# Block 0 of the input projection: raw x tiles transposed as they land, its tokens' norm factors applied behind PSUM, w_in rows loaded by halves

## What is computed

```python
def rmsnorm(x, g):
    r = lax.rsqrt(jnp.mean(xf * xf, axis=-1, keepdims=True) + EPS)
    return (xf * r * g).astype(x.dtype)

h = rmsnorm(x, norm1_g)
z = h @ w_in
za = z[..., :A_WIDTH]      # four Fourier heads
zb = z[..., A_WIDTH:]      # four pooling groups, windows 2, 4, 8, 16
```

## Time and profile before

| | us |
|---|---|
| median of 3 runs | 2491.86 (2491.79 to 2493.97) |
| profiled execution, device time | 2491.23 |
| its span in the trace | 2489.4 |
| PE busy | 2474.7 (99%) |
| DVE busy | 1676.6 (67%) |
| ACT busy | 965.2 (39%) |
| POOL busy | 166.9 (7%) |

### The profile page before, as it was taken

The page is one execution under the profiler, slowest core; times in us unless marked ns, Lnnn a source line. Parts: engine busy times, 40 slices in busy tenths (PEclk is TensorE's granted clock), DMA queues, the critical chain, the costliest instruction groups (busy, mean ns, idle before and its releaser), DMA issues.

```text
span 2489.4 us, 32156 instructions
## 1 busy us (share of the span) xinstructions
PE 2474.7 (99%) x11141; PEld 2049.1 (82%) x11141; DVE 1676.6 (67%) x2600; ACT 965.2 (39%) x1830; POOL 166.9 (7%) x222
## 2 busy tenths in 40 slices
PE   9999999999999999999999999999999999999998
PEld 7888878887888888888888888888888888888887
DVE  5555788779767767877677687666774564455565
ACT  5534566667333333433333343333332232233333
POOL 2555400000000000000000000000000000000000
PEclk9999999999999999999999999999999999999999
DMA  6433767666423222532232432232346654354554
GB/s 184 115 85 99 223 221 254 238 238 260 157 80 116 97 103 110 195 113 110 80 126 101 155 146 96 110 110 89 118 186 217 242 200 168 119 196 149 195 189 148
DMA packets 154373, 381.99 MB, mean 153 GB/s; under 512 B 11992, under 2 KB 48184, under 8 KB 145076
## 3 DMA queue, kind: packets, MB, share of 16 engines
q1 hardware_dynamic: 145616, 350.81, 40.8%
q0 software_dynamic: 8240, 29.94, 3.2%
q10 hardware_dynamic: 432, 0.14, 0.0%
HBM read 254.22 MB, written 126.62 MB: 153 GB/s over the span
## 4 chain that ended last, share of the span: by engine, by line
PE 85%; DVE 2%; ACT 1%; issue 0%; DMA 0%; DVEq 0%
PE bank L351 28%; PE bank L353 28%; PE bank L352 28%; PE bank L2020 1%; ACT a_hi L2401 0%; DVE a_lo L2592 0%; DMA a_raw<-ha_scr 0%; PE bank L1373 0%; PE bank L1059 0%; DVE x L1818 0%; ACT h_out L1637 0%; DVE scratch L1033 0%; DVE zy_late L1044 0%; DVE uv_lo L1071 0%; ACT xn L1627 0%
## 5 line engine op out<-in xcount | busy, mean ns | idle before, releaser
L351 PE MATMUL bank<-a_hi,w_hi 128*128 128x512 f32 x1848 | 719.4, 389 | 2.0 <-DVE w_lo L2603 1.6
L352 PE MATMUL bank<-a_lo,w_hi 128*128 128x512 f32 x1848 | 718.9, 389 | 0.0
L353 PE MATMUL bank<-a_hi,w_lo 128*128 128x512 f32 x1848 | 718.9, 389 | 0.0
L351 PEld LDWEIGHTS bank<-a_hi,w_hi 128*128 128x128 f32 x1848 | 346.9, 188 | 75.6 <-DVE w_lo L2603 2.8
L353 PEld LDWEIGHTS bank<-a_hi,w_lo 128*128 128x128 f32 x1848 | 347.0, 188 | 72.0
L352 PEld LDWEIGHTS bank<-a_lo,w_hi 128*128 128x128 f32 x1848 | 347.0, 188 | 71.7
L351 PE MATMUL bank<-t_hi,s_hi 128*128 128x512 f32 x924 | 359.4, 389 | 0.0
L352 PE MATMUL bank<-t_lo,s_hi 128*128 128x512 f32 x924 | 359.4, 389 | 0.0
L353 PE MATMUL bank<-t_hi,s_lo 128*128 128x512 f32 x924 | 359.4, 389 | 0.0
L2414 ACT ACTIVATE w_hi<-t_raw 128x512 fp32r<-128x512 f32 x256 | 162.3, 634 | 462.4 <-PE bank L353 378.8
L2753 DVE TENSOR_TENSOR s_lo<-s_raw,s_hi 128x512 fp32r<-128x512 f32 x231 | 156.2, 687 | 230.7 <-ACT s_hi L2489 230.7
(11 more groups left out here) (277 smaller groups left out, 3163.1 us busy)
## 6 DMA issues: line engine op xcount, KB each, us to landing
s_scr<-sums_out SPq DMA_DIRECT2D x33, 1792.0 KB, 5.9
s_raw<-s_scr SPq DMA_DIRECT2D x42, 1024.0 KB, 5.0
w_raw<-in_w_gate SPq DMA_DIRECT2D x64, 512.0 KB, 3.5
w_raw<-in_w_up SPq DMA_DIRECT2D x64, 512.0 KB, 4.3
wd_staged<-in_w_down SPq DMA_DIRECT2D x121, 256.0 KB
a_raw<-ha_scr SPq DMA_DIRECT2D x21, 1024.0 KB, 5.0
s_raw<-s_scr SPq DMA_DIRECT2D x21, 768.0 KB, 4.4
x<-in_x SPq DMA_DIRECT2D x24, 512.0 KB, 4.9
```

Source lines behind the costliest of these rows:

```text
L351: pe.matmul(out, w_hi, m_hi, start=first, stop=False, **checks)
L352: pe.matmul(out, w_hi, m_lo, start=False, stop=False, **checks)
L353: return pe.matmul(out, w_lo, m_hi, start=False, stop=last, **checks)
```

## The change

The tiles of block 0 are transposed as they land, without a factor. Each token's factor is applied to z when it leaves PSUM: DVE does this in `first_staged`, in place of ACT's `stage_z(0, c)`. Since a token is a column there, the 512 factors must lie along the free dimension on all partitions: POOL stores `rstd` to a scratch in DRAM and loads it back to all partitions as `rstd_row`. The rows of w_in are loaded by halves, all the pooling halves first, then all the Fourier halves, then x block 1. DVE rounds the first pooling row in ACT's place. Of block 1, ACT scales two quarters in place of one. The squares of tile 3 move behind step d = 1 and the chain of `rstd` behind d = 4.

```diff
         for d in range(KT):
-            sp.dma_start(w_raw[:, d, :], w_rows[d // ROWS, d % ROWS]).then_inc(ahead.row_loaded[d], DMA)
-            if d == 5:
-                load_x(1, 1)
+            sp.dma_start(w_raw[:, d, HALF:], w_rows[d // ROWS, d % ROWS, :, HALF:]).then_inc(ahead.row_loaded[d], DMA)
+        for d in range(KT):
+            sp.dma_start(w_raw[:, d, 0:HALF], w_rows[d // ROWS, d % ROWS, :, 0:HALF]).then_inc(mixed_loaded, DMA)
+        load_x(1, 1)
         sp.dma_start(edges[:, :], edge).then_inc(edge_loaded, DMA)
+        sp.wait_ge(squares_done, 4)
         sp.wait_ge(transposed, KT)
...
+        pool.wait_ge(rstd_chain, 4)
+        pool.dma_start(rstd_scr.rearrange("(p t) -> p t", p=P), rstd[:, 0, :]).then_inc(rstd_moved, DMA)
+        pool.wait_ge(rstd_moved, DMA)
+        pool.dma_start(rstd_row[:, :], rstd_scr.partition_broadcast(P)).then_inc(rstd_moved, DMA)
         pool.wait_ge(edge_loaded, DMA)
...
-        first_squares()
+        for t in range(3):
+            first_squares(t)
+        act.wait_ge(constants_made, GAIN_MADE)
         for d in range(KT):
-            act.wait_ge(ahead.row_loaded[d], DMA)
-            act.activation(w_hi[:, POOLED, d, :], w_raw[:, d, HALF:].rearrange("p (g e) -> p g e", g=4),
-                           ACT.Copy).then_inc(w_hi_done, 1)
...
+            if d:
+                act.wait_ge(ahead.row_loaded[d], DMA)
+                if d == 1:
+                    act.wait_ge(w_hi_done, 1)
+                act.activation(w_hi[:, POOLED, d, :], w_raw[:, d, HALF:].rearrange("p (g e) -> p g e", g=4),
+                               ACT.Copy).then_inc(w_hi_done, 1)
             round_h(0, 0, d, first=True)
+            if d == 1:
+                first_squares(3)
+            if d == 3:
+                act.wait_ge(var_ready, 1)
+                act.activation(std[:, 0, :], var[:, 0, :], ACT.Sqrt).then_inc(std_ready, 1)
-        stage_z(0, 0, first=True)
         for k in range(KT):
             round_folded(k)
             if k < 6:
-                squares(1, 2 * ROWS * DMA, 1, range(4 + 2 * k, 6 + 2 * k))
-            else:
-                stage_z(0, k - 5, first=True)
-        stage_z(0, 3, first=True)
+                squares(1, 2 * ROWS * DMA, 1, range((0, 3, 6, 9, 12, 14)[k], (3, 6, 9, 12, 14, 16)[k]))
...
+        def first_staged(c):
+
+            dve.wait_ge(z_ready, c + 1)
+            if c == 0:
+                dve.wait_ge(rstd_moved, 2 * DMA)
...
+            ps, row = by_tile(z_ps[c % 4][:, :]), rstd_row[:, :].rearrange("q (p t) -> q t p", t=4)
+            if c >= HEADS:
+                h = c - HEADS
+                if h >= 2:
+                    dve.wait_ge(z_stored[h - 2], DMA)
+                dve.tensor_tensor(by_tile(z_out[:, h % 2, :]), ps, row, ALU.mult).then_inc(z_staged, 1)
+                return
+            staged = dve.tensor_tensor(by_tile(zb[:, c, 2 * PAD:2 * PAD + HALF]), ps, row, ALU.mult)
+            if c:
+                staged = dve.scalar_tensor_tensor(out=by_tile(zk[:, c - 1, PAD:WIDE]), in0=ps, scalar=float(WINDOWS[c]),
+                                                  in1=row, op0=ALU.mult, op1=ALU.mult)
+            staged.then_inc(z_staged, 1)
...
         copy_turned(0)
+        first_staged(0)
         for k in range(KT):
             if k + 1 < KT:
                 copy_turned(k + 1)
             rest_of_folded(k)
-        step(0, 0, quarters=3)
+            if k + 1 < HEADS:
+                first_staged(k + 1)
+        first_step()
...
         pe.wait_ge(warm_ready, 2)
-        pe.wait_ge(x_first[0], DMA)
-        warm_up(4)
+        warm_up(7)
         pe.wait_ge(const_loaded, DMA)
...
+        for t in range(4):
+            pe.wait_ge(x_first[t], DMA)
             for d in range(4):
...
                 mm = pe.transpose(t_ps[d][:, t * P:(t + 1) * P], every_fourth(xin[0][:, t, :], d), eye[:, :])
+                if t == 3:
+                    mm.then_inc(transposed, 1)
+            if t == 1:
+                pe.wait_ge(constants_made, DMA)
+                for r in range(ROWS):
...
+            if t:
+                warm_up(1)
```

More of the change, by code:

```diff
@@ L371, in every_fourth, with project_in @@
     return ap.rearrange("p (s j r) -> p s r j", s=2, r=ROWS)[:, d // ROWS, d % ROWS]
-def project_in(nc, ctx, ahead, mixer, pooled, x, w_in, g1, ident, z_scr, table, channel, edge):
+def project_in(nc, ctx, ahead, mixer, pooled, x, w_in, g1, ident, z_scr, rstd_scr, table, channel, edge):
     NJ = TOKENS // HALF
@@ L493, in scalar, with first_squares @@
     def scalar(act):
[L494 to L504, removed]
+        def first_squares(t):
+            act.wait_ge(x_first[t], DMA)
+            if t:
+                act.wait_ge(squares_done, t)
+            act.activation(junk[:, :], xin[0][:, t, :], ACT.Square,
+                           accum_out=sumsq[:, 0, t:t + 1]).then_inc(squares_done, 1)
         def squares(j, loads, slot, blocks=range(NBLK)):
@@ L530, in stage_z @@
                     act.wait_ge(z_stored[h - 2], (j + 1) * DMA)
-                elif not first:
+                else:
                     act.wait_ge(z_stored[h + 2], j * DMA)
@@ L535, in stage_z @@
             g = c
-            if not first:
-                act.wait_ge(ahead.group_done, j * 4 + (g - 3))
+            act.wait_ge(ahead.group_done, j * 4 + (g - 3))
             staged = act.activation(zb[:, g, 2 * PAD:2 * PAD + HALF], z_ps[c % 4][:, :], ACT.Copy)
@@ L657, in rest_of_folded, with step @@
                               w_hi[:, MIXED, k, :].bitcast(F32), ALU.subtract).then_inc(w_ready, 1)
-        def step(j, slot, quarters=4):
-            norm(j + 1, 1 - slot, quarters)
+        def step(j, slot):
+            blocks_variance(j + 1)
+            blocks_scale(j + 1, 1 - slot, 4)
             for d in range(3):
@@ L666, in step, with first_step @@
                     turn(j + 1, 1 - slot, d + 3)
+        def first_step():
+            blocks_variance(1)
+            first_staged(HEADS)
+            blocks_scale(1, 1, 2)
+            for d in range(3):
+                turn(1, 1, d)
+                if d == 1:
+                    first_staged(HEADS + 1)
+            for d in range(KT):
+                rest_of_h(1, 1, d)
+                if d + 3 < KT:
+                    turn(1, 1, d + 3)
+                if d == 3:
+                    first_staged(HEADS + 2)
+            first_staged(HEADS + 3)
         dve.memset(warm[:, 0:1], 1.0).then_inc(warm_ready, 1)
         dve.memset(ahead.still[:, :].bitcast(F32), 0.0).then_inc(warm_ready, 1)
[L670 to L675 removed]
         dve.wait_ge(constants_made, GAIN_TURNED)
@@ L680, in vector @@
                             ).then_inc(constants_made, 1)
+        dve.wait_ge(ahead.row_loaded[0], DMA)
+        dve.tensor_copy(w_hi[:, POOLED, 0, :], w_raw[:, 0, HALF:].rearrange("p (g e) -> p g e", g=4)).then_inc(w_hi_done, 1)
         dve.wait_ge(constants_made, GAIN_MADE)
@@ L747, in turn_w @@
         def turn_w(k):
+            if k == 0:
+                pe.wait_ge(mixed_loaded, (KT + 1) * DMA)
             if k < 2:
@@ L3023, in encoder @@
         pooled = Pooled(ahead, y_scr)
-        front = project_in(nc, ctx, ahead, mixer, pooled, x, w_in, g1, ident, z_scr, table, channel, edge)
+        front = project_in(nc, ctx, ahead, mixer, pooled, x, w_in, g1, ident, z_scr, rstd_scr, table, channel, edge)
         mixing = mix(nc, ctx, ahead, mixer, z_scr, y_scr, w_pool)
```

91 lines of the change are left out of this document (36 added, 55 removed).

## The result

The changed kernel takes 2495.44 us (median of 22 runs, 2492.83 to 2498.81) against 2492.39 us for the kernel before (22 runs, 2490.98 to 2494.83): ratio 1.0013, 95% interval 1.0007 to 1.0019. It is 3.05 us slower, where the forecast stood at -0.15 against a baseline of 2491.86; the measured time lies 0.4 us above the range given. The difference is under the 0.2% that was named as the bound of "same", yet its interval excludes zero.

A forecast was written before the change was run, and what follows sets the result against it. PE's unbroken matmul stream was taken as the bound. Terms -2.45 + 2.3 + 0 + 0 = -0.15 against the profiled 2491.23 gave 2491.1, or 2491.7 in the median's terms; range 2489.2 to 2495.0 us.

The forecast's parts named there:

- What bounds the kernel: Whole span: one unbroken PE matmul stream, busy 99%, so only the first product's start and later holes decide.
- Part 1: Start: transposes without the norm bring the first product from 13.56 to 10.8; -2.45 us, from -3.65 to -0.35.
- floor of 9.9: Start: earliest first product, set by tile 3 alone and row 0's copy; 9.9, or -3.65.
- rival (c): Start: PE is slow at its first products; -0.35 + 2.3, 2493.8 us; chance 0.13.
- Part 2: Folds: DVE staging pair at 1.28 us delays fold 2 by 1.28, then two slips of 0.5; +2.3 us.
- break-even of 1.34 a pair: Folds: staging pair price above which the sum of fold slips and the start's -2.45 exceeds zero.
- Part 3: Factors' way through DRAM: two POOL DMAs at 3.0 us each land by 25.7, 8 us of cover; cost 0.
- Part 4: first_step of block 1: chain grows by 1.45 us, some 1.7 returns from POOL's earlier groups; 0, or +1.2 without return.
- The rule on GpSimd: Staged operations, bank and row, are free of POOL's contention; if false, 0.4 each, up to 2 us more.
- (b): Folds: staged pair costs more than it looks, counted three times; +3.65, 2495.5 us at doubled price; chance 0.12.
- signs of being wrong: Folds show no hole, the pair costs above 2 us, or the first product stays behind 12.
- the floor of part 1: Start: part 1's best case, -3.65 us, said to be left out of the range.

The follow-up runs named there:

- warm10: Changed kernel with ten dummy matmuls in place of seven ahead of the transposes; 2494.39 us, ratio 1.0007 to the kernel before.
- x_behind_warm: x_behind_store with ten dummy matmuls in place of seven; 2489.45 us, ratio 0.9989 to the kernel before.
- start_alone: Changed kernel with ACT copying z out of PSUM as before, block 0's factors and their DMAs left out; 2489.19 us, ratio 0.9990 to the kernel before.
- hole_filled: Changed kernel with dummy matmuls (7, 4 and 4) ahead of folds 2, 3 and 4; 2496.79 us, ratio 1.0013 to the kernel before.
- row_flat: Changed kernel reading the factors from adjacent words instead of every fourth, so they go to wrong tokens; 2492.38 us, ratio 1.0001 to the kernel before.
- x_behind_store: both_mended with x block 1 loaded only once the factors' store has landed; 2491.07 us, ratio 0.9993 to the kernel before.
- factors_first: both_mended with x block 1's load issued only when both factor DMAs have landed; 2492.34 us, ratio 0.9995 to the kernel before.
- both_mended: folds_mended with block 1's scaling put before the fifth group's staging in first_step; 2491.51 us, ratio 0.9992 to the kernel before.
- changed_again: Changed kernel unaltered, run again for a second profile; 2496.06 us, ratio 1.0011 to the kernel before.
- staging_alone: Kernel before with only DVE's staging by first_staged, using a row of ones; 2497.89 us, ratio 1.0024 to the kernel before.
- folds_mended: Changed kernel with one DVE staging operation per group, ACT making zk, three of four staged before the folds; 2492.18 us, ratio 1.0000 to the kernel before.

## Why the forecast was wrong

**What bounds the kernel** held. PE is busy 99% of the span, and up to the last `row_sums` the difference of every version is found in its start and its holes. Behind that mark all programs are the same, and the profiles need 2270.7 to 2272.6 us there (2274.3 in the first of the changed kernel). With such a scatter in single executions the medians follow the marks only to 1 or 2 us.

**Part 1** was right in mechanism, too large in this kernel. The terms up to `eye` held: the first transpose at 6.30, 0.40 before the 6.70 of the earlier trace rows. The term that failed is the price of the transposes: 0.12 each from the earlier trace rows, 0.24 each measured (8 in 1.91), then 0.18 for the next eight. That is 0.96 + 0.46 us, and the two dummies between them took 0.3 more than 0.43 each: the first product stands at 12.01 in place of 10.8 in spite of the 0.4 gained. Those prices were read behind a run of dummy matmuls; here PE had paused from 4.9 to 6.3. With that pause filled the transposes cost 0.145 each and the first product is at 10.03 and 10.02 (`warm10`, `x_behind_warm`), near the floor of 9.9 that the text gave. The pause does not decide alone: `start_alone` and `hole_filled` paused too, did the first eight in 1.16 and slowed only then (10.94 and 11.13). The forecast did think of PE's speed, but put it only on the products (rival (c)); there it cost 0.2 us (3.04 us for the twelve of d = 0, 2.84 before). By d = 1 the start brought 1.35 in place of 2.45; in `start_alone`, with its better pass, 2.4.

**Part 2** is the step that failed, by the size of one term: the pair of staged operations, put at 1.28 us, takes 1.97. Its structure held to the tenth: fold 2 slips by one pair, folds 3 and 4 each by the pair less 0.79. At the forecast's 1.28 that was +2.3. `row_flat` measured 1.19, just under the neighbour rows' price, and 1.19 + 2 x 0.40 = 2.0 is what its folds cost (36.79 - 34.83). With the stride the pair is 1.97, and the same formula gives 1.97 + 2 x 1.18 = 4.3; the trace shows 4.2 at fold 4 and 4.3 at the first `row_sums`. The text had the stride as a doubt, with its own upper value of 2.56 and the break-even of 1.34 a pair, and gave that side a chance of 0.12, on the ground that one element per lane and cycle seemed to be DVE's pace in all rows. But no row that it showed had a strided operand, so they could not speak for it. The trace of the kernel before had one, in DVE's turns of block 1 (L636), which read x at every fourth word too:

```profile
63.97 1.08 DVE L636 STREAM_TRANSPOSE x_turned<-xin 128x512 f32<-128x512 f32 x1
64.99 1.06 DVE L642 SCALAR_TENSOR_TENSOR h_lo<-x_turned,gain,h_hi 128x512 fp32r<-128x512 f32 x1
```

It takes 1.02 us from start to start. It is another instruction, so the row doesn't prove the price of a staged operation, but it contradicts one pace for all rows. The Trainium skill has the rule that the forecast overlooked: "SBUF — State Buffer", section Door 1: The DMA port swizzle, says that SBUF is read in lines of 16 bytes and that each access to a new line pays a penalty. The factors stood exactly 16 bytes apart, one line each; the measured 0.98 against 0.60 us agrees. No run tried another stride, so that the line is what sets the price is not shown; that the stride does is.

**Part 3** came out at the forecast's cost of zero, but by luck: of the 8 us of cover 0.7 was left, and behind it DVE's idle 1.9, which the forecast did not count. The terms were two DMAs at 3.0, taken from a store of POOL elsewhere; they took 8.0 and 5.3, close to the bound of 8.5 for the first. The DMA engines were moving x block 1 in small runs at 205 GB/s at that moment, which the forecast itself had computed (landing by 30 to 40), and did not set beside the store at 20.9. `x_behind_store`, with nothing ahead of the store (0 GB/s from 20 to 21 us), shows 2.0. `factors_first` and `x_behind_warm` have 1.9. The Trainium skill, "DMA: Bandwidth & Descriptors", section Queues, rings and completion order, says that a DMA's semaphore increment on an engine lands only after every earlier write of that engine, across its queues; 8.0 behind a full queue and 1.9 to 2.0 behind an empty one agree with it. No run here shows the order inside an engine, so whether the store's data or only its report was late stays open.

**Part 4** was taken as 0, with 1.2 if GpSimd's return fails; it cost 1.0 (0.67 of it the wait for `h_lo`), 1.4 in the second profile. The terms for the scaling (2.36 for two quarters on DVE, 3.31 for ACT's eight) held. What was missed is again the stride: three staged operations ahead of the last `h_lo` at 0.98 are 1.1 us more than at 0.61. `row_flat` shows 167.45 between the `row_sums` and no wait, so at the flat price the 0 was right. `both_mended` has the same 167.45 with the stride, by the order of the operations alone.

**The rule on GpSimd** stood the test. The staged operations read one bank and one row of SBUF; the first, at 35.20 with GpSimd idle, took 1.05, and those at 42.54 and 43.52, beside a window sum of GpSimd, 1.07 and 1.10. Nothing of the 0.4 each that was the price if the rule were false.

Of the rivals (b) is what happened, at less than its full price: +4.3 + 1.0 - 1.35 = +3.95 by terms, +4.0 by the mark at 222.73, +3.05 by the medians. The 0.9 between the last two is within what executions of one kernel differ by (6 us from lowest to highest of the 22). Of the forecast's own signs of being wrong, the first product behind 12 came true by a hair (12.01), and the pair above 2 us failed by one (1.97).

One sum of the range was off as well: it was said to leave out the floor of part 1, but that floor alone, -3.65 + 2.3, gives 2490.5 in the median's terms, inside the range.

## What to carry to other kernels

Price an operand by its own access pattern: a row with a contiguous operand says nothing of one that takes every fourth word, and an operation put into a loop that DVE already bounds is paid once per iteration. If a table can be laid flat when it is written, do that. A small DMA whose landing someone needs lands late behind bulk traffic in short runs. Holding the bulk back until the store had landed brought the factors 7 us forward, but no time here, where DVE then waited for ACT; holding it back until the load had landed as well cost 1 us. When the work ahead of the first product is cut, look at what PE does in the pause that the cut opens. And when profiles of single executions are compared, count from a mark behind the part that scatters: here the start moved by 1.3 us between executions of the same program, and the bare marks would credit an edit in the folds with it.

## What was not expected of the hardware

- DVE with an fp32 operand in SBUF at a stride of 16 bytes: 0.98 us for 128x512 from start to start, 0.60 flat, for tensor_tensor and scalar_tensor_tensor alike.
- A store of 2 KB took 8.0 us beside 512-byte runs at 205 GB/s (7.6 in `changed_again`, 8.5 in `warm10`), and 1.9 to 2.0 without them.
- PE's granted clock fell to 0.50 (the lower of its two levels, 1.2 GHz) between 43 and 46 us, behind an idle stretch of 1.91 us in the folds; with dummies in that stretch it stayed at 1.00. `changed_again` (44 to 47 us) and `staging_alone` (44 to 47) show the same fall behind 1.90 and 1.91. But in `warm10` it stayed at 1.00 behind an idle stretch of 1.91 as well, so the stretch alone doesn't decide it. The fall in the folds, where DVE set the pace, cost nothing.
- At the start the records of the granted clock and the pace disagree: in the changed kernel the transposes of 6.30 take 0.24 us each, in `warm10` 0.145, while the windows of both read 1.00. In `start_alone` the transposes went at the upper pace, and the windows then read 0.54 and 0.50 at 8 to 11 us:

```profile
8.00:9.00 1.00, 1.00 (x5) 0.88 (x6) 0.62 (x4) 0.54 (x2) 0.22 (x6) 0.54 1.00 348
9.00:10.00 1.00, 1.00 (x5) 0.83 (x4) 0.59 (x2) 0.00 (x0) 0.84 (x10) 0.50 1.07 401
```

  Its eight later transposes, in that stretch, took 0.18 each, as in the changed kernel. Why the level differs between executions in the first 10 us was not tried.
- GpSimd and DVE give way to each other when DVE has two SBUF operands, and which of the two pays varies: in `folds_mended` DVE's scaling of two quarters took 3.24 us instead of 2.36, in the changed kernel it kept its 2.36 and GpSimd's window sum behind it took 2.17 instead of 1.31.
